# A seventeenth home for the experts' weights: the buffer of transposed rows becomes one, and the last gate row goes by DRAM

## The chip, the core and the metric

The kernel is one program on one core of a Trainium2 chip. The metric is device time in microseconds (us) of one execution, the median of three runs. A profiled execution, taken apart, gives the rows below. The engines are TensorE (PE; PEld is its weight load), VectorE (DVE), ScalarE (ACT), GpSimd (POOL) and SyncE (SP), which here issues nothing but DMAs.

## The reference, cut to what matters

Two layers of a diffusion transformer over 256 tokens of 1024 channels, all in float32. The even layer is attention with Fourier channel groups and then a dense SwiGLU; the odd layer is a gated short convolution and then eight expert SwiGLUs, of which each token uses two:

```
probs = softmax(h @ router); vals, idx = top_k(probs, 2); wts = vals / sum(vals)
combine = sum(one_hot(idx, 8) * wts[..., None], axis=-2)
for e in range(8):
    out = out + combine[..., e:e+1] * ((silu(h @ w_gate[e]) * (h @ w_up[e])) @ w_down[e])   # 1024 x 3584, 3584 x 1024
x = x + gate2 * rmsnorm(out, g_post)
```

The last line needs a "gate row": the modulation gate times the norm's weight, 1024 numbers, the same for every token. All of the experts' weights are read once: 8 experts of 42 MB (here and below 1 MB is 2^20 bytes, 128 partitions by 8 KB).

## The kernel before, in words

**The stream.** All weights lie in DRAM as units of 2 MB (128 partitions by 4096 floats) in the order of their use. SP loads them one after the other. In the dense layers a unit goes into one of the seven slots of `ring`. An expert has 21 units: 14 of gate and up weights (`gate_up`), then 7 of down weights (`down`). Here units are split in halves of 1 MB, p0 to p41, and each half has a *home*: `HOME[p]`. Homes 0 to 13 are the halves of the ring's seven slots; homes 14 and 15 lie in `wide_acc`, a buffer that the dense layers use for other things. `home_at` gives a home's place.

**How a home comes free.** TensorE signals `given_back[home]` when it has used a half: for the even half in the middle of the unit's work, for the odd half with the first matmul of the next unit. SP waits for `given_back` of a home before it loads the next half into it (L438 in the expert loop), strictly in the order p0, p1, ... Nothing later can go ahead of a half whose home is still in use. The table says which half of the expert used the home before. With 16 homes the table is 0 to 15, then 0 to 3, 6 to 15, 4, 5, 6 to 15: so p20 (home 6) waits for p6, p30 (home 4) for p4, p32 (home 6) for p20. Units listed in `BY_HALVES` are loaded by two DMAs of 1 MB (L413) and TensorE waits for each half apart; all others by one DMA of 2 MB (L410), which waits for both homes and for which TensorE waits at the start of the unit. Before, units 7, 8, 14, 19 and 20 go by halves.

**The experts.** The number of tokens of an expert selects the width of its code: 64, 96, 128, 144 and so on (`ARMS`). Each width has its own unrolled code; after each expert TensorE branches to the next width's code. With the inputs of this case the tiles in the trace show the widths 64, 96, 144, 64, 128, 64, 96, 64 for experts 0 to 7. Widths 64 and 96 are "narrow": tokens are the stationary side (L1953 for gate and up, L1995 for down). Wider ones keep the weights stationary (L1928). ACT computes silu into `gated_e` (L760) and DVE multiplies it with the up half (L1316). `gated_e` is the first 1024 floats of `hT`; `hT` (2048 floats per partition, exactly one home) otherwise holds the transposed rows of the layer's input, whose last reader is the router's matmul (semaphore `logit_ps`, L1806).

**The gate rows.** `gg` is the last 2048 floats of `wide_acc`: gate rows for the third and the fourth norm. The first of them is read in `add_y(2, b)` before the experts begin, the second in `add_y(3, b)` at the very end (L1030). Home 15 overlaps the first.

**Order around the change.** Home 14's first load waits for `red_ps` 13, home 15's for the gather matmuls (`gather_ps` 4), with which the experts begin. During an expert POOL fetches the next one's rows; in the last expert it fetches the experts' results from `y_store`, in two steps (`fetch_results`, L541).

## Time and profile before

| | us |
|---|---|
| median of 3 runs | 1436.09 (1435.29 to 1437.74) |
| the profiled execution | 1438.39 |
| its span, first to last instruction | 1436.6 |
| PE busy | 1387.9 (97%) |
| weight load busy | 979.0 (68%) |
| DVE, ACT, POOL busy | 462.6, 269.3, 49.2 |
| moved by DMA | 490.45 MB, mean 341 GB/s |

PE is shown busy nearly all the time, but its ends are modelled: a PE that is paced by the weights' arrival looks busy too. The waits of PE, the rate of the DMA engines and the moments at which SP issues the loads say more. The experts take the time from 522.6 to about 1425 us.

### The profile page before, as it was taken

To read this page: it belongs to the slowest core of one execution; us is meant where nothing else is said; L and a number is where in the kernel's file an instruction comes from. 1 tells how busy PE (TensorE), PEld (TensorE's weight loads), DVE (VectorE), ACT (ScalarE), POOL (GpSimd) and SP (SyncE) were. 2 spreads that over 40 slices of the span, in tenths; PEclk is the share of its full clock that TensorE was granted. 3 is DMA by queue.
4 is the path that set the end of the run, shared out by engine and by line. 5 is a ranking of instruction groups with operands and counts; after the bars stand their busy time and mean duration, and the time that the engine had idled before them with its cause. 6 is when DMAs were issued, how large, how long until landed. Compare 5 with 4: busy or idle time off the path is not lost.

```text
span 1436.6 us, 24598 instructions
## 1 busy us (share of the span) xinstructions
PE 1387.9 (97%) x10446; PEld 979.0 (68%) x10446; DVE 462.6 (32%) x759; ACT 269.3 (19%) x557; POOL 49.2 (3%) x63
## 2 busy tenths in 40 slices
PE   7999999998999999899999999999999999999896
PEld 4456599973598576366489954658994795664782
DVE  3587787777477341111000000101000111110122
ACT  3245321110300132111110000311000221110221
POOL 1000000000100012000000000000000000000000
PEclk9999999999999999999999999999999999999998
DMA  9977766660698679999996587999979999999995
GB/s 380 383 298 292 267 233 238 257 237 0 270 427 343 257 270 421 423 424 425 417 416 243 216 323 286 386 424 426 425 278 396 381 426 425 424 415 419 423 425 237
DMA packets 47531, 490.45 MB, mean 341 GB/s; under 512 B 7091, under 2 KB 7827, under 8 KB 13888
## 3 DMA queue, kind: packets, MB, share of 16 engines
q1 hardware_dynamic: 39136, 468.96, 80.0%
q0 software_dynamic: 6624, 17.08, 3.1%
q10 hardware_dynamic: 1664, 2.75, 0.5%
q8 instruction: 95, 1.56, 0.4%
q14 instruction: 12, 0.10, 0.0%
HBM read 480.83 MB, written 13.26 MB: 344 GB/s over the span
## 4 chain that ended last, share of the span: by engine, by line
PE 85%; DMA 8%; DVE 4%; ACT 1%; issue 1%; SPq 0%; DVEq 0%; ACTq 0%
PE ps L1953 24%; PE ps L1928 15%; PE ps L1995 14%; PE ps L1629 9%; DMA ring<-stream 7%; PE ps L1742 5%; PE ps L1665 4%; PE ps L1394 3%; PE ps L1576 2%; DMA hTe<-ctx_in 2%; PE ps L1911 1%; DVE acc L885 1%; PE ps L1494 1%; PE ps L1456 1%; PE ps L1510 1%
## 5 line engine op out<-in xcount | busy, mean ns | idle before, releaser
L1953 PE MATMUL ps<-ring,hTe 128*64 128x256 f32 (+1 forms) x3328 | 339.7, 383 | 13.5 <-issue 9.4
L1953 PEld LDWEIGHTS ps<-ring,hTe 128*64 128x64 f32 (+1 forms) x3328 | 234.4, 131 | 99.2 <-issue 23.6
L1316 DVE TENSOR_TENSOR aT<-hT,ps 128x512 f32<-128x512 f32 x112 | 77.1, 688 | 547.1 <-ACT hT L760 541.4
L1995 PE MATMUL ps<-ring,aT 128*32 128x256 f32 (+2 forms) x1120 | 207.3, 507 | 4.9 <-DMA ring<-stream 4.9
L1928 PE MATMUL ps<-hTe,ring 128*128 128x144 f32 (+1 forms) x1664 | 195.7, 281 | 2.1 <-DMA ring<-stream 2.1
L1928 PEld LDWEIGHTS ps<-hTe,ring 128*128 128x128 f32 x1664 | 195.1, 191 | 3.8 <-DMA ring<-stream 3.0
L1995 PEld LDWEIGHTS ps<-ring,aT 128*32 128x32 f32 (+2 forms) x1120 | 82.0, 133 | 122.7 <-issue 104.8
L760 ACT ACTIVATE hT<-ps 128x512 f32<-128x512 f32 x112 | 66.9, 597 | 458.5 <-PE ps L1953 273.6
L885 DVE SCALAR_TENSOR_TENSOR acc<-ring,silu_c,acc 128x1024 f32<-128x1024 f32 x80 | 102.6, 1282 | 2.9 <-DMA ring<-stream 0.9
L1742 PE MATMUL ps<-hT,ring 128*128 128x256 f32 (+1 forms) x480 | 83.9, 337 | 0.0
L1995 PE MATMUL ps<-acc,aT 128*64 128x512 f32 (+2 forms) x448 | 83.4, 503 | 0.0
L1742 PEld LDWEIGHTS ps<-hT,ring 128*128 128x128 f32 x480 | 76.2, 191 | 7.9 <-issue 0.5
L1258 DVE TENSOR_SCALAR hTe<-ps,ab 128x256 f32<-128x256 f32 x28 | 13.3, 537 | 188.8 <-PE ps L1840 188.8
L1629 PE MATMUL ps<-hT,ring 128*128 128x128 f32 x528 | 61.2, 275 | 0.2 <-issue 0.2
L1995 PEld LDWEIGHTS ps<-acc,aT 128*64 128x64 f32 (+2 forms) x448 | 32.9, 133 | 41.7 <-issue 38.1
L1629 PEld LDWEIGHTS ps<-hT,ring 128*128 128x128 f32 x528 | 60.0, 192 | 1.0 <-issue 1.0
L753 ACT ACTIVATE aT<-ps 128x512 f32<-128x512 f32 x84 | 49.8, 593 | 17.5 <-PE ps L1911 17.4
L731 ACT ACTIVATE hTe<-ps,ab 128x256 f32<-128x256 f32 x28 | 13.5, 564 | 167.7 <-PE ps L1840 167.7
L1629 PE MATMUL ps<-xn,acc 128*128 128x128 f32 x352 | 43.0, 275 | 0.6 <-DVE xn L1016 0.6
L1629 PE MATMUL ps<-xn,ring 128*128 128x128 f32 x352 | 43.0, 275 | 0.0
L1911 PE MATMUL ps<-cst,aT 128*64 128x128 f32 (+1 forms) x448 | 42.2, 273 | 0.0
L1394 PE MATMUL ps<-ring,hT 128*128 128x512 f32 x96 | 42.1, 593 | 0.0
(278 smaller groups left out, 1129.6 us busy)
## 6 DMA issues: line engine op xcount, KB each, us to landing
ring<-stream SPq DMA_DIRECT2D x182, 2048.0 KB, 14.8
acc<-stream SPq DMA_DIRECT2D x48, 1024.0 KB, 16.6
ring<-stream SPq DMA_DIRECT2D x32, 1024.0 KB, 16.1
y_store<-aT POOLq DMA_DIRECT2D x1, 8192.0 KB, 28.2
acc<-norm_w POOLq DMA_DIRECT2D x4, 512.0 KB, 18.2
y_store<-acc ACTq DMA_DIRECT2D x10, 128.0 KB, 9.3
x<-x_in SPq DMA_DIRECT2D x1, 1024.0 KB, 5.3
hTe<-ctx_in SPq DMA_DIRECT2D x1, 1024.0 KB, 22.9
```

The costliest lines, as they stand in the source:

```text
L753: act.activation(aT_e[:, u, :, :].rearrange("p b n -> p (b n)"), ps[:, 6 + u % 2, :], ACT.Copy).then_inc(eT_ok, 1)
L760: act.activation(gated_e[:, u % 2, :, :], ps[:, q:q + 2, 0:SEQ], ACT.Silu).then_inc(e_silu, 1)
L885: last = dve.scalar_tensor_tensor(out=dst, in0=slot(what)[:, k * D:(k + 1) * D][:, cols], scalar=silu_c[:, 4 * h + k, 0:1], in1=dst, op0=A ...
L1316: dve.tensor_tensor(aT_e[:, u, :, :], gated_e[:, u % 2, :, :], ps[:, q:q + 2, SEQ:2 * SEQ], ALU.mult).then_inc(e_a, 1)
L1394: last = pe.matmul(ps[:, blk, :], lhs[:, k, b * P:(b + 1) * P], w[:, k, :], start=(k == 0), stop=(k == KD - 1))
L1629: last = pe.matmul(ps[:, gu_bank(u, x), i * P:(i + 1) * P], w[:, i, k * P:(k + 1) * P], tokens[:, k, :], start=(x in (1, 2, 5, 7) and i == ...
L1665: last = pe.matmul(ps[:, bank, :], lhs[:, k, :], w[:, k, :], start=(d == 0 and k == 0), stop=(d == DOWNS - 1 and k == n - 1))
L1742: last = pe.matmul(ps[:, bank, c + t0:c + t1], w[:, i % 4, k, :], hT[:, k, t0:t1], start=(k == 0), stop=(k == KD - 1))
L1911: last = pe.matmul(ps[c:c + tile, 6 + u % 2, b * 256:b * 256 + P], aT_e[:, u, b, c:c + tile], ident, start=True, stop=True)
L1928: last = pe.matmul(ps[:, 2 * (u % 2) + b, g * SEQ:g * SEQ + width], w, hTe[:, k, 0:width], start=(k == 0), stop=(k == KD - 1))
L1953: last = pe.matmul(to, hTe[:, k, s0:s0 + n], w, start=(k == 0), stop=(k == KD - 1))
L1995: last = pe.matmul(ps[n * r:n * (r + 1), bank, 0:cols], a_T, w[:, part * cols:(part + 1) * cols], start=(j == 0), stop=(j == NFE - 1))
```

## The change

Seventeen homes. Homes 0 to 13 stay; home 14 stays; home 15 is now `hT` as a whole; home 16 is the former home 15. `gated_e` moves from `hT` to the last 1024 floats of `wide_acc`, where the fourth norm's gate row was. That row is therefore written to DRAM (`gate_store`) once it is ready, and read back, broadcast to all partitions (512 KB), into the place of home 0 in the last expert, after home 0's last use. ACT waits once for the write before its expert loop. The table of homes is new: 0 to 16, then 0 to 3, 9 to 16, 4 to 8, 9 to 16. Because 17 is odd, pairs of homes no longer fall on whole units: now units 4, 7, 8, 9, 10 and 13 to 20 go by halves, 13 of 21 in place of 5.

```diff
-HOME = [0, 1, 2, 3, 4, 5, 6, 7, 8, 9, 10, 11, 12, 13, 14, 15,
-        0, 1, 2, 3, 6, 7, 8, 9, 10, 11, 12, 13, 14, 15, 4, 5,
-        6, 7, 8, 9, 10, 11, 12, 13, 14, 15]
+HOME = [0, 1, 2, 3, 4, 5, 6, 7, 8, 9, 10, 11, 12, 13, 14, 15, 16,
+        0, 1, 2, 3, 9, 10, 11, 12, 13, 14, 15, 16, 4, 5, 6, 7, 8,
+        9, 10, 11, 12, 13, 14, 15, 16]
...
-BY_HALVES = [u for u in range(PER_EXPERT) if HOME[2 * u] >= 2 * RING or u in (2 * RING // 2 + 1, PER_EXPERT - 2)]
+BY_HALVES = [u for u in range(PER_EXPERT)
+             if HOME[2 * u] % 2 or HOME[2 * u + 1] != HOME[2 * u] + 1 or HOME[2 * u + 1] >= 2 * RING
+             or STAYS[HOME[2 * u]] != STAYS[HOME[2 * u + 1]]]
...
-        gated_e = hT[:, 0:4, :].rearrange("p (r k) t -> p r k t", r=2)
+        gated_e = wide_acc[:, 7 * D:8 * D].rearrange("p (r k t) -> p r k t", r=2, k=2)
...
         def home_at(home):
+            if home == 2 * RING + 1:
+                return hT[:, :, :].rearrange("p k t -> p (k t)")
             if home >= 2 * RING:
-                at = (0, 5 * D)[home - 2 * RING]
+                at = 0 if home == 2 * RING else 5 * D
...
+        last_gate = home_at(0)[:, 0:D]
...
                 elif home == 2 * RING:
                     sp.wait_ge(red_ps, 13)
+                elif home == 2 * RING + 1:
+                    sp.wait_ge(logit_ps, 2)
...
+            pool.wait_ge(red_ok, 10)
+            pool.dma_start(gate_store, gg[0:1, 1, :]).then_inc(gate_kept, 16)
...
             fetch_results(y_sum, 0, y_back)
+            pool.wait_ge(given_back[0], E * STAYS[0])
+            pool.wait_ge(gate_kept, 16)
+            pool.dma_start(last_gate, gate_store.to_broadcast([P, D])).then_inc(gate_back, 16)
             pool.wait_ge(e_ps, E * GU_UNITS)
             fetch_results(y_more, 1, y_more_back)
...
+            act.wait_ge(gate_kept, 16)
...
+                gates = last_gate if post == 3 else gg[:, post % 2, :]
+                if post == 3 and b == 0:
+                    dve.wait_ge(gate_back, 16)
```

Two places of the program show how the order moves. The first is SP in expert 0, from p16 on (the loop over the later experts has the same order). Before, `given_back6` and `given_back7` are waited for by p20 and p21, `given_back10` and `11` by p24 and p25:

```order
L413 DMA ring<-stream 128x2048 [waits given_back0]
L413 DMA ring<-stream 128x2048 [waits given_back1]
L410 DMA ring<-stream 128x4096 [waits given_back3,given_back2]
L410 DMA ring<-stream 128x4096 [waits given_back7,given_back6]
L410 DMA ring<-stream 128x4096 [waits given_back9,given_back8]
L410 DMA ring<-stream 128x4096 [waits given_back11,given_back10]
L410 DMA ring<-stream 128x4096 [waits given_back13,given_back12]
L413 DMA acc<-stream 128x2048 [waits given_back14]
L413 DMA acc<-stream 128x2048 [waits given_back15]
L410 DMA ring<-stream 128x4096 [waits given_back5,given_back4]
```

The same place with the change, from p16 on; `given_back15` is now `hT` and `given_back16` the second home in `wide_acc`:

```order
L420 DMA acc<-stream 128x2048 [waits gather_ps,rows_free]
L420 DMA ring<-stream 128x2048 [waits given_back0]
L420 DMA ring<-stream 128x2048 [waits given_back1]
L420 DMA ring<-stream 128x2048 [waits given_back2]
L420 DMA ring<-stream 128x2048 [waits given_back3]
L420 DMA ring<-stream 128x2048 [waits given_back9]
L417 DMA ring<-stream 128x4096 [waits given_back11,given_back10]
L417 DMA ring<-stream 128x4096 [waits given_back13,given_back12]
L420 DMA acc<-stream 128x2048 [waits given_back14]
L420 DMA hT<-stream 128x2048 [waits given_back15]
L420 DMA acc<-stream 128x2048 [waits given_back16]
L420 DMA ring<-stream 128x2048 [waits given_back4]
```

The row behind `given_back3` waits for home 9 now (p21 for p9), where before it was home 6 (p20 for p6); homes 4 to 8, free by then, are only loaded from p29 on. The row that waits for homes 10 and 11 loads p22 and p23 now, and loaded p24 and p25 before.

The second place is POOL at the end of the program, before and with the change. `xn` takes the first results, `hTe` the second:

```order
L541 DMA xn<-y_store,row_at 128x1024 [waits returned,gather_ps]
L541 DMA xn<-y_store,row_at 128x1024
L541 DMA hTe<-y_store,row_at 128x1024 [waits e_ps]
L541 DMA hTe<-y_store,row_at 128x1024
L139 UNCONDITIONAL_BRANCH
```

```order
L552 DMA xn<-y_store,row_at 128x1024 [waits returned,gather_ps]
L552 DMA xn<-y_store,row_at 128x1024
L562 DMA ring<-gate_store 128x1024 [waits gate_kept,given_back0]
L552 DMA hTe<-y_store,row_at 128x1024 [waits e_ps]
L552 DMA hTe<-y_store,row_at 128x1024
```

The gate row's read stands between the two fetches, behind home 0's last use (p17, in unit 8 of the last expert).

## Rows read from the trace of the kernel before

**Rows 1.** PE's waits in the whole span, longest in total first.

```profile
PE ps L1953 <- issue: 9.4, 3, 3.7
...
PE ps L1995 <- DMA ring<-stream: 4.9, 4, 2.0
PE ps L1953 <- DMA ring<-stream: 4.1, 1, 4.1
...
PE ps L1928 <- DMA ring<-stream: 2.1, 1, 2.1
```

**Rows 2.** Busy time, clock, DMA share, GB/s in windows, one an expert.

```profile
core 0: us, PE busy (x) PEld busy (x) DVE busy (x) ACT busy (x) POOL busy (x), PEclk, DMA share, GB/s
522.60:600.80 78.20, 77.81 (x632) 44.88 (x632) 15.27 (x35) 18.60 (x34) 15.69 (x24) 1.00 0.98 392
605.00:725.80 120.80, 120.80 (x1361) 66.95 (x1362) 12.92 (x20) 18.80 (x34) 1.99 (x2) 0.99 1.00 422
725.80:899.60 173.80, 173.80 (x1250) 138.81 (x1252) 12.92 (x20) 12.77 (x21) 1.98 (x2) 1.00 0.74 289
899.60:977.20 77.60, 77.60 (x632) 44.64 (x632) 12.82 (x20) 19.73 (x35) 1.98 (x2) 1.00 1.00 416
979.30:1129.50 150.20, 150.18 (x1026) 123.07 (x1028) 12.83 (x20) 12.07 (x21) 1.99 (x2) 1.00 0.93 377
1129.50:1207.20 77.70, 77.70 (x632) 64.96 (x632) 12.73 (x20) 19.71 (x35) 1.98 (x2) 1.00 1.00 417
1210.20:1330.80 120.60, 120.56 (x1360) 66.78 (x1360) 12.92 (x20) 19.01 (x34) 0.00 (x0) 0.99 1.00 420
1334.50:1425.00 90.50, 83.37 (x624) 63.35 (x624) 15.61 (x22) 17.19 (x30) 3.78 (x4) 0.96 0.93 392
```

**Rows 3.** The chain that ended last: three expert boundaries and the end.

```profile
578.15 26.00 DMA ring<-stream
604.15 0.83 issue
...
955.48 23.79 DMA ring<-stream
979.32 0.71 PE ps L1928 x4
...
1185.45 23.25 DMA ring<-stream
1208.70 1.53 issue
...
1387.29 23.86 DMA ring<-stream
1411.19 3.65 PE ps L1995 x16
```

**Rows 4.** SP's issues at the start of expert 5 (start, us, count).

```profile
1137.38 0.33 SPq L410 DMA_DIRECT2D ring<-stream  x1
...
1144.73 0.33 SPq L410 DMA_DIRECT2D ring<-stream  x1
1148.39 7.68 SPq L410 DMA_DIRECT2D ring<-stream  x3
```

**Rows 5.** Issue to landing (us) of p24/p25: windows 545.0:545.2, 922:923, 1152:1153.

```profile
ring<-stream SPq DMA_DIRECT2D x1, 2048.0 KB, 13.2
...
ring<-stream SPq DMA_DIRECT2D x1, 2048.0 KB, 12.7
...
ring<-stream SPq DMA_DIRECT2D x1, 2048.0 KB, 11.7
```

**Rows 6.** The same for lone transfers: windows 757:766, 1122.5:1123, 1083.5:1093.

```profile
ring<-stream SPq DMA_DIRECT2D x2, 2048.0 KB, 9.3
...
ring<-stream SPq DMA_DIRECT2D x1, 2048.0 KB, 9.0
...
acc<-stream SPq DMA_DIRECT2D x2, 1024.0 KB, 5.1
```

**Rows 7.** Totals of windows 1223:1232 (2 MB loads) and 1240.3:1244.8 (1 MB loads).

```profile
DMA packets 262, 3.85 MB, mean 428 GB/s; under 512 B 27, under 2 KB 27, under 8 KB 27
...
DMA packets 260, 1.89 MB, mean 421 GB/s; under 512 B 29, under 2 KB 29, under 8 KB 29
```

**Rows 8.** Windows of 10 us early in expert 5 and late in expert 6.

```profile
1140.00:1150.00 10.00, 10.00 (x102) 9.95 (x100) 2.06 (x3) 3.25 (x6) 0.00 (x0) 1.00 1.03 435
1150.00:1160.00 10.00, 10.00 (x102) 9.95 (x100) 2.04 (x3) 3.26 (x6) 0.00 (x0) 1.00 1.00 426
1290.00:1300.00 10.00, 10.00 (x92) 3.81 (x84) 0.69 (x1) 1.68 (x3) 0.00 (x0) 1.00 0.92 365
1300.00:1310.00 10.00, 10.00 (x94) 3.87 (x93) 0.00 (x0) 0.00 (x0) 0.00 (x0) 1.00 1.03 433
```

**Rows 9.** PE in the last expert's last three units.

```profile
1411.19 3.65 PE L1995 MATMUL ps<-ring,aT 128*64 128x512 f32 x16 [1.62 <-DMA ring<-stream]
1414.77 3.70 PE L2014 MATMUL ps<-xn,cst 128*128 128x512 f32 x8
1418.40 3.65 PE L1995 MATMUL ps<-ring,aT 128*64 128x512 f32 x16
1421.89 3.60 PE L1995 MATMUL ps<-acc,aT 128*64 128x512 f32 x16
```

**Rows 10.** PE's waits for "issue" where the last expert begins.

```profile
1334.52 2.80 PE L1953 MATMUL ps<-ring,hTe 128*64 128x256 f32 x22 [3.70 <-issue]
1339.96 6.17 PE L1953 MATMUL ps<-ring,hTe 128*64 128x256 f32 x41 [2.65 <-issue]
```

More of the change, by code:

```diff
@@ L167, in build @@
         y_store = nc.dram_tensor("y_store", (SEQ * E, D), F32).ap()
+        gate_store = nc.dram_tensor("gate_store", (1, D), F32).ap()
         slot_table = nc.dram_tensor("slot_table", (SEQ * E, 2), F32).ap()
@@ L272, in build @@
             sem(n) for n in ("table_empty", "entries_ok", "table_s", "rows_out", "lists_in", "token_at_ok", "rows_back"))
-        stored = sem("stored")
+        stored, gate_kept, gate_back = sem("stored"), sem("gate_kept"), sem("gate_back")
         gu_done, gu_sum, snap, c_ok = sem("gu_done"), sem("gu_sum"), sem("snap"), sem("c_ok")
@@ L1029, in add_y @@
                     cols = slice(h * BANK, (h + 1) * BANK)
-                    dve.tensor_tensor(xn[:, b, cols], y_bank(post, b)[:, h, :], gg[:, post % 2, cols], ALU.mult)
+                    dve.tensor_tensor(xn[:, b, cols], y_bank(post, b)[:, h, :], gates[:, cols], ALU.mult)
                 roots[0] += 1
```

## The prediction, made before the changed kernel ran

> **What bounds the kernel now.** I read PE's waits first [rows 1]. In 1436.6 us it waits for weights by name only 4.9 + 4.1 + 2.1 = 11.1 us, and 9.4 us for "issue". Then a window for each expert [rows 2]: the reader is to see two kinds. In experts 2 (width 144) and 4 (width 128) the DMA engines move 289 and 377 GB/s while PE works without a gap: PE sets the pace, and SP waits for homes. In the others they move 416 to 422 GB/s at a DMA share of 1.00 (experts 0 and 7, at 392, contain their own ramp and end). A width-64 expert takes PE about 77.7 us for 42 MB, that is 1.85 us a MB, but 2^20 bytes at 425 GB/s take 2.47 us: there the weights fall behind by some 26 us, which the loaded homes have to cover. The chain of waits [rows 3] shows that they just do not: at the ends of experts 0, 3 and 5 it goes through a weight DMA and the next expert starts late (at 979.32 straight from a landing, at 604.15 and 1208.70 a landing plus 0.83 and 1.53 us of issue), and in the last expert it goes through a landing at 1411.15. So there are three stretches in which every microsecond of delay of the weights is a microsecond of the kernel: A, expert 0 up to the start of 1; B, expert 3 up to the start of 4; C, from expert 5 to the end. Elsewhere PE is the bound and more homes change nothing.
>
> **What 17 homes ought to give.** One more MB loaded when a stretch begins is 2.47 us of DMA time, three times: 7.4 us. Whether it reaches the stretch's end depends on whether the DMA engines stay busy in between, and this is where the new table matters.
>
> **The table at the start of a width-64 expert.** Both tables load the first expert's halves without waiting for one another; then PE eats faster than homes refill. Before, p20/p21 wait for p6/p7, issued at 1144.73 [rows 4], and the next three 2 MB loads are issued from 1148.39 on at (7.68 - 0.33) / 2 = 3.67 us apart: 1148.39 (homes 8, 9), 1152.06 (homes 10, 11), 1155.73 (homes 12, 13). These are the moments at which PE frees those homes, and they don't move. Now p21 alone waits for home 9, 1148.39; p22/p23 wait for homes 10 and 11, 1152.06; p24/p25 for homes 12 and 13, 1155.73. Each is 2 MB further back in the stream than what stood there before, and homes 4 to 8 lie empty until p29. By 1149 the engines have nothing left: before, p18/p19, issued at 1137.38 [rows 4], land like p24/p25 some 11.7 us later [rows 5], at about 1149; now the seventeenth home lets the engines start 1 MB earlier, which puts p20, the last before p21, at about the same moment. So p21 runs alone, landing 5.1 us after issue [rows 6] at 1153.5, and p22/p23, issued 1.4 us before that, are almost alone too: 9.3 us to landing, 1161.4, then p24/p25 one transfer of 2 MB later: 2 x 2.444 = 4.89 us by the 428 GB/s of [rows 7] (1.0486 / 0.428 = 2.45 us a MB). From the same issue moment that is 9.3 + 4.9 = 14.2 us, against 13.2, 12.7 and 11.7 us measured for p24/p25 in experts 0, 3 and 5 [rows 5]. The same half of the stream lands **1.0, 1.5 and 2.5 us later** than before, in spite of the extra home. With the lone transfer at 9.0 us (the other row in [rows 6]) it is 0.3 us less each. From there to the stretch's end the engines run without a break in both kernels, so the difference stays. As bounds: if p20 to p23 in fact queue up and none is lone, nothing is lost and up to 2.5 us a stretch gained; if p22/p23 start only when p21 has landed (1153.5 + 9.3 + 4.9 = 1167.7 against 1163.8), 3.9 us are lost.
>
> **More transfers of 1 MB.** Thirteen units by halves in place of five: 16 MB more of each expert in 8 KB rows. 1 MB costs 1.0486/0.421 = 2.49 us so, and 2.45 in 2 MB loads [rows 7]; with the rounding of the rates 0.04 to 0.05. Of the tail of a stretch (p26 to p41) 10 MB change form: 0.5 us in A, 0.5 in B, 0.5 in C for expert 5; all of experts 6 and 7 adds 0.8 each. C: 2.1 us. Bounds 0 and twice that.
>
> The Trainium skill ("DMA: Bandwidth & Descriptors", section "Anatomy of one DMA") puts a fixed cost of about 2.0 us on each DMA beside its bytes. Taken one by one that would be 8 x 2.0 = 16 us an expert. The trace has it for a lone load (5.1 us for 1 MB, 9.3 for 2 MB, [rows 6]), but in a full queue a row of 1 MB loads still moves 421 GB/s [rows 7], so it is covered there; it is only paid where the queue runs dry, which is the step above.
>
> **The gap in expert 6.** At 1290 to 1300 the rate is 365 GB/s [rows 8], 10 x (1 - 365/425) = 1.4 us of idle: p36/p37 waited there for the pair of units 12/13. Now p36 waits for p23, a pair earlier; the gap goes: **-1.4 us** (bounds 0 and -1.4).
>
> **The gate row.** Its write (4 KB) is issued by POOL between two issues that wait far apart, ACT waits for it long after; nothing. The read moves 512 KB into SBUF while stretch C's weights run: 0.524 MB at 425 GB/s = **+1.2 us** on the stream's end (it is issued when unit 9 begins, about 1372). The second result fetch behind it on POOL waits for the end of gate and up, 1387, so isn't held up. What if PE's last units had slack: then 0, the lower bound.
>
> **Finer waits at the end.** PE now waits for p36 at unit 18 and for p37 half a unit later. The wait that ends at 1411.19 [rows 9] was for a whole unit; half of that unit's work, 3.65 / 2 = 1.8 us, now goes ahead of the landing. Behind it stand 3.6 + 3.6 + 3.6 us without a wait, and the last half was due at 1421.89 + 1.8: the last landing then becomes equally tight. **-1.8 us** (bounds 0 and -1.8). Units 0, for which the starts of experts 1, 4 and 6 wait, are whole in both.
>
> **Others at nothing.** `gated_e` elsewhere: the same ACT and DVE instructions. Home 15 can be filled from `logit_ps` on (before the gathers): its 2.5 us lie in a DMA pause, and this is the extra MB of stretch A already counted. PE's code grows by a net one instruction for each width.
>
> **Sum.** A: 1.0 + 0.5 = 1.5. B: 1.5 + 0.5 = 2.0. C: 2.5 + 2.1 - 1.4 + 1.2 - 1.8 = 2.6. Together +6.1; with the lone transfer at 9.0 us, 0.9 less: +5.2. In A part of the delay may hide in the 0.83 us of issue behind the landing. I take **+5.1 us**. The profiled execution took 1438.39 us (span 1436.6 and 1.8 around it), which becomes 1443.5; the median of the runs, 2.3 us below the profiled one, goes from 1436.09 to **1441.2**. A measurement of this kernel can tell about 0.2%, 2.9 us, from no change.
>
> **Rival 1: the extra home pays (faster).** If the engines don't run dry at p21, each stretch gains 2.47 us less the packets: A -2.0, B -1.6 (its wait was 2.1 in all, less 0.5), C -2.5 + 2.1 - 1.4 + 1.2 - 1.8 = -2.4: 1430.1. For it speak the waits, which exist; against it, that the issue moments of [rows 4] are PE's, and the new order reads from the table. It would decide where p20 lands later than 1150. Chance 0.14.
>
> **Rival 2: they cancel.** The delay at p24/p25 is nearer 0 to 1 us, because traffic that slows the weights in the first 15 us of an expert (results stored, rows gathered) now falls into the idle time: A 0.5, B 0.5, C 0.5 + 2.1 - 1.4 + 1.2 - 1.8 = 0.6: +1.6, 1437.7. For it: p24/p25 in expert 0, where most such traffic is, comes out as the smallest delay. Chance 0.24.
>
> **Rival 3: code loading (much slower).** PE waits 3.70 and 2.65 us for "issue" as the last expert begins [rows 10], neither for a landing. The change shifts the code by an instruction per width and adds halves' waits. A pause of 3.7 us more at each of the three starts 1, 4 and 6 would give 5.1 + 11.1: 1452.3. Against it: experts 3 and 5 start without any pause, and the pauses lie at branches that are the same. The Trainium skill ("Runtime: NRT & Kernel Launch", "Instruction fetch mechanics") says that a taken branch out of the loaded blocks waits for a fetch of the target; the pauses at the last expert agree, and by that rule an instruction more changes nothing unless a block's edge is crossed. Chance 0.06.
>
> **How the numbers follow.** Forecast 0.56, rivals 0.14, 0.24, 0.06. The forecast's own range is 1438 to 1446 (the lost time 0.3 us less or 1.4 us more a stretch, the packets 0 or double). For 8 in 10 I go from 1433.5 to 1446.5: it leaves out the far half of rival 1, rival 3 and the forecast's upper edge. Slower by over 2.9 us (1439.0): 0.51 of the forecast, rival 3 and 0.04 of rival 2: 0.61. Same: the rest of the forecast 0.05, 0.19 of rival 2 and 0.03 of rival 1: 0.27. Faster: 0.12.
>
> **What the profile after would show.** At the start of experts 3 and 5: SP issues a 1 MB load some 18.9 us after the expert's start, then 2 MB loads 3.67 us apart; in the windows of 10 us there, a rate 20 to 30% below 425 between 14 and 24 us after the start, where 435 and 426 stand in [rows 8]; p24/p25 landing about 14 us after issue. PE's wait at the start of expert 4 near 4 us in place of 2.1. No dip late in expert 6. A wait of PE in the last units of experts 0, 3 and 5. The prediction is wrong if that dip is absent or if the start waits of experts 1, 4 and 6 shrink; wrong in its size if p24/p25 lands within 12 to 13 us.

## The result

| us | before | changed |
|---|---|---|
| median | 1436.91 (4 runs, 1435.29 to 1438.31) | 1447.62 (4 runs, 1447.37 to 1450.86) |
| the profiled execution | 1438.39 | 1447.71 |
| its span | 1436.6 | 1445.9 |

The ratio is 1.0074, 95% interval 1.0058 to 1.0089: 10.7 us slower. The forecast was +5.1 us and its range ended at 1446.5: the direction was right, the size was not.

PE's waits after, to be read against [rows 1] ("issue" is time in which PE waited for nothing that the profile shows):

```profile
PE ps L1971 <- issue: 11.3, 4, 4.8
...
PE ps L1971 <- DMA ring<-stream: 5.1, 1, 5.1
PE ps L2013 <- DMA ring<-stream: 4.5, 5, 1.8
PE ps L1946 <- DMA ring<-stream: 3.5, 1, 3.5
```

L1971, L2013 and L1946 are the former L1953, L1995 and L1928. Each of the three waits at an expert's start has grown: 4.1 to 5.1 at expert 1, 2.1 to 3.5 at expert 4, and 3.0 to 4.8 (put down to issue) at expert 6. One window for each expert, as in [rows 2]:

```profile
522.90:600.80 77.90, 77.67 (x633) 44.77 (x632) 15.25 (x35) 18.68 (x34) 15.69 (x24) 1.00 0.95 374
606.10:726.80 120.70, 120.66 (x1361) 66.95 (x1361) 12.92 (x20) 17.85 (x33) 1.98 (x2) 0.99 1.01 422
...
900.70:978.90 78.20, 77.61 (x632) 44.56 (x632) 12.81 (x20) 19.72 (x35) 1.97 (x2) 1.00 0.97 394
982.90:1135.50 152.60, 152.60 (x1024) 125.53 (x1024) 12.82 (x20) 11.69 (x20) 1.98 (x2) 0.98 0.93 371
1135.50:1215.10 79.60, 78.41 (x633) 60.97 (x632) 12.82 (x20) 19.71 (x35) 1.98 (x2) 1.00 0.97 395
```

The reader is to see the last column: in experts 0, 3 and 5 the rate fell from 392, 416 and 417 GB/s to 374, 394 and 395. The weights are the bound there and the DMA engines now stand still for part of the time. The row of expert 4 tells something else: 152.6 us in place of 150.2 with a mean clock of 0.98.

SP's issues at the start of expert 5, as in [rows 4]. The row x5 ends with p21 (20.5 us after the start; 19.2 in expert 3), the row x2 is p22 to p25:

```profile
1138.09 18.26 SPq L420 DMA_DIRECT2D ring<-stream  x5
1159.74 4.00 SPq L417 DMA_DIRECT2D ring<-stream  x2
1165.09 0.33 SPq L420 DMA_DIRECT2D acc<-stream  x1
```

Windows of 10 us there (15 us behind the start) and late in expert 6, against [rows 8]:

```profile
1150.50:1160.50 10.00, 10.00 (x102) 9.11 (x100) 2.06 (x3) 3.26 (x6) 0.00 (x0) 1.00 0.73 275
...
1300.00:1310.00 10.00, 10.00 (x91) 3.84 (x84) 0.69 (x1) 1.68 (x3) 0.00 (x0) 1.00 1.01 419
```

The dry spell that was forecast is there (275 GB/s), and the gap late in expert 6 is gone. The same 10 us of experts 0 and 3 are alike, the kernel before first and then the changed one:

```profile
537.50:547.50 10.00, 10.00 (x100) 6.86 (x98) 2.06 (x3) 2.79 (x6) 3.19 (x6) 1.00 1.01 428
914.50:924.50 10.00, 10.00 (x100) 6.82 (x98) 2.06 (x3) 2.81 (x6) 0.00 (x0) 1.00 1.01 433
```
```profile
537.90:547.90 10.00, 10.00 (x100) 6.82 (x98) 2.06 (x3) 2.78 (x6) 5.56 (x11) 1.00 0.65 224
915.60:925.60 10.00, 10.00 (x100) 6.82 (x98) 2.06 (x3) 3.01 (x6) 0.00 (x0) 1.00 0.77 269
```

In the last expert PE waits by halves, as against [rows 9]:

```profile
1417.30 1.94 PE L2013 MATMUL ps<-ring,aT 128*64 128x512 f32 x8 [0.54 <-DMA ring<-stream]
1419.79 1.94 PE L2013 MATMUL ps<-ring,aT 128*64 128x512 f32 x8 [0.55 <-DMA ring<-stream]
1422.25 1.94 PE L2013 MATMUL ps<-ring,aT 128*64 128x512 f32 x8 [0.53 <-DMA ring<-stream]
```

Two things were not forecast. Early in expert 5 PE stands after 22 matmuls, in the middle of a unit, for no landing:

```profile
1135.54 2.80 PE L1971 MATMUL ps<-ring,hTe 128*64 128x256 f32 x22
1139.54 4.69 PE L1971 MATMUL ps<-ring,hTe 128*64 128x256 f32 x41 [1.20 <-issue]
```

Unit 2's first matmul comes 8.9 us after the expert's start, where it was 7.3: 1.6 us later, and so are the homes that come free behind it. And at the start of expert 4, behind the wait of 3.5 us, the granted clock is 0.50 (the lower level, 1.2 GHz). Windows of 2 us:

```profile
982.00:984.00 2.00, 1.12 (x5) 1.12 (x6) 0.00 (x0) 1.28 (x1) 0.00 (x0) 0.50 1.01 419
...
986.00:988.00 2.00, 2.00 (x12) 2.00 (x11) 0.00 (x0) 0.00 (x0) 0.00 (x0) 0.50 1.03 431
988.00:990.00 2.00, 2.00 (x18) 2.00 (x18) 0.00 (x0) 0.00 (x0) 0.00 (x0) 0.91 1.02 432
```

The spell lasts from 981.5 to 988.4, and 5.5 us of it lie behind the first matmul of expert 4 (982.9). Work at half the clock for 5.5 us loses 2.7: that is the 2.6 us by which expert 4 is longer (start to start 152.7 against 150.1).

### The profile page after: what moved, and what is told of

Its sections match the earlier page's. It is cut to its first block, busy times and chain, and to the rows that moved or that the text cites. A ratio compares the mean times of both kernels' runs of the same rounds, so it can differ in the third digit from the quotient of the medians.

```text
span 1445.9 us, 24722 instructions
## 1 busy us (share of the span) xinstructions
PE 1392.4 (96%) x10446; PEld 977.9 (68%) x10446; DVE 462.7 (32%) x759; ACT 269.2 (19%) x557; POOL 50.3 (3%) x65
## 4 chain that ended last, share of the span: by engine, by line
PE 84%; DMA 9%; DVE 4%; ACT 1%; issue 1%; SPq 0%; DVEq 0%; ACTq 0%
PE ps L1971 24%; PE ps L1946 15%; PE ps L2013 14%; PE ps L1647 9%; DMA ring<-stream 7%; PE ps L1760 5%; PE ps L1683 4%; PE ps L1412 3%; PE ps L1594 2%; DMA hTe<-ctx_in 2%; PE ps L1929 1%; DVE acc L900 1%; PE ps L1512 1%; PE ps L1474 1%; PE ps L1528 1%
## 5 line engine op out<-in xcount | busy, mean ns | idle before, releaser
L1971 PE MATMUL ps<-ring,hTe 128*64 128x256 f32 (+1 forms) x2944 | 309.7, 385 | 16.4 <-issue 11.3
L1971 PEld LDWEIGHTS ps<-ring,hTe 128*64 128x64 f32 (+1 forms) x2944 | 208.6, 132 | 98.2 <-issue 25.9
L1334 DVE TENSOR_TENSOR aT<-acc,ps 128x512 f32<-128x512 f32 x112 | 77.0, 688 | 553.5 <-ACT acc L775 550.7
L2013 PE MATMUL ps<-ring,aT 128*32 128x256 f32 (+2 forms) x1120 | 208.7, 504 | 4.5 <-DMA ring<-stream 4.5
L1946 PE MATMUL ps<-hTe,ring 128*128 128x144 f32 (+1 forms) x1472 | 176.8, 283 | 3.5 <-DMA ring<-stream 3.5
L1946 PEld LDWEIGHTS ps<-hTe,ring 128*128 128x128 f32 x1472 | 175.7, 193 | 5.1 <-DMA ring<-stream 4.3
L2013 PEld LDWEIGHTS ps<-ring,aT 128*32 128x32 f32 (+2 forms) x1120 | 82.4, 133 | 120.7 <-issue 97.3
L775 ACT ACTIVATE acc<-ps 128x512 f32<-128x512 f32 x112 | 66.9, 597 | 469.8 <-PE ps L1971 279.8
L2013 PE MATMUL ps<-acc,aT 128*64 128x512 f32 (+2 forms) x336 | 66.8, 503 | 0.8 <-DMA acc<-stream 0.8
L768 ACT ACTIVATE aT<-ps 128x512 f32<-128x512 f32 x84 | 49.8, 593 | 17.5 <-PE ps L1929 17.4
L1971 PE MATMUL ps<-acc,hTe 128*64 128x256 f32 (+1 forms) x384 | 47.5, 380 | 0.0
L2013 PEld LDWEIGHTS ps<-acc,aT 128*64 128x64 f32 (+2 forms) x336 | 24.0, 133 | 33.0 <-issue 26.7
```

The source lines that it names most:

```text
L768: act.activation(aT_e[:, u, :, :].rearrange("p b n -> p (b n)"), ps[:, 6 + u % 2, :], ACT.Copy).then_inc(eT_ok, 1)
L775: act.activation(gated_e[:, u % 2, :, :], ps[:, q:q + 2, 0:SEQ], ACT.Silu).then_inc(e_silu, 1)
L1334: dve.tensor_tensor(aT_e[:, u, :, :], gated_e[:, u % 2, :, :], ps[:, q:q + 2, SEQ:2 * SEQ], ALU.mult).then_inc(e_a, 1)
L1946: last = pe.matmul(ps[:, 2 * (u % 2) + b, g * SEQ:g * SEQ + width], w, hTe[:, k, 0:width], start=(k == 0), stop=(k == KD - 1))
L1971: last = pe.matmul(to, hTe[:, k, s0:s0 + n], w, start=(k == 0), stop=(k == KD - 1))
L2013: last = pe.matmul(ps[n * r:n * (r + 1), bank, 0:cols], a_T, w[:, part * cols:(part + 1) * cols], start=(j == 0), stop=(j == NFE - 1))
```

## The experiments

Differences are from the median of the kernel before in the same comparison, which lay at 1436.7 to 1438.7 us; ratios are of the runs of the kernel to the runs of the kernel before, with their 95% interval. The changed kernel is +10.7. In the diffs + and - are against the changed kernel where nothing else is said. Its `BY_HALVES` is worked out from `HOME`, so a new table also changes which units go by halves: 13 of them in the changed kernel, 3 in a16, 15 in k1, 13 in k2, 14 in c17 and 15 in t17.

### Is it the table? a16, bhalf, anogate, lighta, lightb

**a16**:

```diff
-HOME = [0, ..., 16, 0, 1, 2, 3, 9, ..., 16, 4, ..., 8, 9, ..., 16]
+HOME = [0, ..., 15, 0, 1, 2, 3, 6, ..., 15, 4, 5, 6, ..., 15]
```

> The changed kernel with the table of sixteen homes of the kernel before; the second home outside the ring is hT, and the gate row still goes by DRAM. Theory (the table alone is the cause): as the kernel before plus 1.2 us of the gate row's read, 1438.1 us, 1436.5 to 1439.5; start of expert 4 with a wait of about 2 us and no spell at clock 0.50; expert 5 begins without a pause for issue. Rival (the gate row, hT as a home or the shifted code cost): 1442 us or more, with the pause at the start of expert 5.

1440.19 us, +2.3; 1.0015 (1.0000 to 1.0030). The table, with the halving that follows from it, takes 8.4 of the 10.7 us away. A little above the expected range. In its trace PE stands 3.48 us at the start of expert 4, put down to issue, where the two profiles of the kernel before wait 2.1 and 1.6 us for weights; there is no pause in expert 5.

**bhalf** (against the kernel before):

```diff
-BY_HALVES = [u for u in range(PER_EXPERT) if HOME[2 * u] >= 2 * RING or ...]
+BY_HALVES = [4, 7, 8, 9, 10, *range(13, 21)]
```

> The kernel before, its table kept, with 13 units by halves in place of 5 (units 4, 7 to 10 and 13 to 20), the same as in the changed kernel. Theory (1 MB transfers cost 0.04 to 0.05 us each where the queue is full, and the finer waits at the end give back 1.8): 0.5 + 0.5 + 2.1 - 1.8 = 1.3 us more than before, 1438.2 us, 1436 to 1440. Rival (1 MB transfers carry what the prediction missed): 1442 us or more. If the code's shift by more waits makes the pause in expert 5, it shows here too.

1437.53 us, -0.4; 1.0001 (0.9987 to 1.0015). The 1 MB transfers cost nothing that can be measured, a little less than forecast. No pause in expert 5.

**anogate**:

```diff
-            pool.dma_start(last_gate, gate_store.to_broadcast([P, D])).then_inc(gate_back, 16)
...
-                    dve.wait_ge(gate_back, 16)
```

> The changed kernel without the read of the gate row; the last norm multiplies with whatever lies in home 0, so this part of the output is not the reference's. Theory (the read of 0.5 MB takes 1.2 us of the weights' stream in the last expert): 1446.4 us, 1445 to 1447. Rival (it is hidden): 1447.6. Rival (it costs much more, because it is written to 128 partitions and stands ahead of the second fetch of results): below 1444.

1446.85 us, +9.6; 1.0068 (1.0052 to 1.0085). This kernel leaves out the read of the gate row. Its median is 0.8 us below the changed kernel's (1.1 if each is taken from its own kernel before) where 1.2 was expected; the intervals overlap, so it only shows that the read is not large.

**lightb** and **lighta** (the same edit on the kernel before and on the changed one; every load of the experts' weights leaves out half of its columns):

```diff
-                    sp.dma_start(ring[:, ring_slot(HOME[p]), :], stream[..., :, :],
+                    sp.dma_start(ring[:, ring_slot(HOME[p]), 0:HALF], stream[..., :, 0:HALF],
...
-                sp.dma_start(home_at(HOME[p]),
+                sp.dma_start(home_at(HOME[p])[:, 0:HALF // 2],
```

> The kernel before with the loads of the experts' weights cut to half their columns in the same way; output not the reference's. Theory: 1410 to 1425 us, the same as lighta within 1.5 us; the waits for issue (9.4 us before) shrink where the queue is light. Rival on those waits (they belong to the branches and don't depend on the queue): they stay at 3 us or more each at the starts of experts 1, 6 and 7.

> The changed kernel with every load of the experts' weights cut to half its columns, so half of each expert's weights are old numbers and the output is not the reference's; the same number of DMAs, waits and matmuls. Theory (nothing but the arrival of the weights separates the two kernels): the same time as lightb within 1.5 us; both have no wait for weights in the experts, 1410 to 1425 us; what is left of PE's waits for issue at the starts of experts shows how much of them comes from the loaded queue. Rival (moved buffers, gate row, code): lighta 3 us or more above lightb.

1417.15 and 1416.32 us; 0.9850 (0.9833 to 0.9868) and 0.9847 (0.9829 to 0.9865). With the weights out of the way the two kernels are equal within what can be measured (intervals of 2.6 us to either side): the moved buffers and the code show no cost of their own. PE has no wait for weights in the experts, and its waits for issue in lighta, from 520 us on, are

```profile
PE ps L1971 <- issue: 4.5, 2, 2.8
```

against 11.3 in the changed kernel, and 5.2 in lightb against 9.4. So about 1416 us is what is left when no table makes PE wait for weights, and about half of the waits put down to issue come only beside a full DMA queue.

### Which entry of the table? k1, k2, c17, t17

**k1** and **k2**, one and two homes moved forward:

```diff
-HOME = [*range(17), *range(4), *range(9, 17), *range(4, 9), *range(9, 17)]
+HOME = [*range(17), *range(5), *range(9, 17), *range(5, 9), *range(9, 17)]    # k1
+HOME = [*range(17), *range(6), *range(9, 17), *range(6, 9), *range(9, 17)]    # k2
```

> The changed kernel with one entry of the table moved: home 4 goes from p29 to p21, and homes 9 to 16 move up by one (0 to 16, 0 to 4, 9 to 16, 5 to 8, 9 to 16). p21 then waits for p4, used long before, and p22 waits for p9. Theory (p21's wait for p9 and the dry spell behind it make the three stretches late): no dry spell, p24/p25 land 2 to 4 us earlier after each start, 1439 us, 1436 to 1442. Rival (seventeen homes cost in any order, through the moved buffers, the gate row or the code): 1445 us or more. Rival (only the wrap from one expert to the next counts, as it did with the table of c17, where p4 waited for p33): no change from 1447.6.

> The same with homes 4 and 5 moved up to p21 and p22 (0 to 16, 0 to 5, 9 to 16, 6 to 8, 9 to 16). Theory: p23 is the first to wait for p9, and by then the engines still have three loads queued; p4 and p5 of the next expert still wait for halves 25 loads back. Each stretch gains something of the seventeenth home over the kernel before: 1436 us, 1433 to 1439. Rival: as k1, 1445 us or more; or equal to the kernel before, 1438.

k1: 1441.90 us, +4.7; 1.0031 (1.0019 to 1.0042). k2: 1436.93 us, -0.3; 0.9999 (0.9990 to 1.0008). One home takes back 6.0 us, two take back 11.0: all of the loss. The halving can't be the reason: k1 sends the same 15 units by halves as a11 below, which has the changed kernel's table and takes 1450.79 us (+12.1), and k2 has 13 such units like the changed kernel (unit 11 for unit 13). The same 10 us of expert 5, from about 15 us behind its start, in k1, in k2:

```profile
1147.90:1157.90 10.00, 10.00 (x102) 9.08 (x100) 1.91 (x3) 3.26 (x6) 0.00 (x0) 1.00 0.98 386
```
```profile
1140.10:1150.10 10.00, 10.00 (x102) 9.06 (x100) 2.06 (x3) 3.26 (x6) 0.00 (x0) 1.00 1.02 424
```

275 GB/s became 386 and then 424, the rate of the kernel before.

**c17**:

```diff
+HOME = [*range(17), 0, 1, 2, 3, *range(4, 12), 12, 13, 14, 15, *range(4, 12), 16]
```

> The changed kernel with another table of seventeen homes: 0 to 16, 0 to 3, 4 to 11, 12 to 15, 4 to 11, 16, so that p21 waits for p4 and every load up to p32 reuses the home of the load 17 before it. Theory (the loss comes from the order of the homes: p21 waits for p9 and the DMA engines run dry there): no dry spell, the seventeenth home pays 2.47 us less the 1 MB transfers in each stretch, PE's wait at the start of expert 4 falls below 1 us and with it the spell at clock 0.50; 1431 us, 1428 to 1434. Rival (the 1 MB transfers, here nearly all, or the gate row are what costs): 1445 us or more. Rival (the seventeenth home is worth nothing in any order): 1437.

1455.44 us, +17.5; 1.0122 (1.0094 to 1.0149): wrong by 24 us. The rival that named such a time, the 1 MB transfers, is not the reason: aall below has more of them (all 21 units, here 14) and takes 1441.30. The table is a ring: behind p41 comes p0. In c17 home 4 is last used by p33, so p4 of the next expert waits for p33, 13 loads back, where in the changed kernel it waited for p29. SP's 2 MB loads at the end of expert 2, in c17 and in the kernel before:

```profile
843.14 55.41 SPq L415 DMA_DIRECT2D ring<-stream  x7
```
```profile
845.68 45.70 SPq L410 DMA_DIRECT2D ring<-stream  x7
```

The seven loads that should be a stock for the width-64 expert take 55.4 us to issue in place of 45.7, and p4/p5 goes out at 868.2 in place of 853.6. The order around p21 was mended and the order across the experts was broken.

**t17**, a table found by counting issue, arrival and use for each half with the durations of the trace:

```diff
+HOME = [*range(17), 0, 1, 2, 4, 3, 6, 7, 8, 11, 10, 14, 15, 16, 1, 12, 4, 5, 9, 8, 10, 11, 13, 14, 15, 16]
```

> The changed kernel with a table found by working the order of homes through a count of issue, arrival and use: 0 to 16, then 0, 1, 2, 4, 3, 6, 7, 8, 11, 10, 14, 15, 16, 1, 12, 4, 5, 9, 8, 10, 11, 13, 14, 15, 16; no home comes back in fewer than 12 loads where the engines could run dry. Theory (more of the seventeenth home's 2.5 us a stretch reaches the end than with k2): by that count 2 us below k2, 1435 us, 1432 to 1438. Rival (at the starts of experts 1, 5, 6 and 7 PE waits for issue anyway, as in k2, so earlier weights give nothing): 1437, as k2 and the kernel before.

1444.74 us, +6.0; 1.0045 (1.0029 to 1.0061): worse than k2, not better. The count knew nothing of waits for issue and clock. t17 has a pause of 3.1 us at the start of expert 2, one of 2.1 in expert 5, and spells at 0.50 that begin at 1400.3 and 1417.3 us, and the down units of its last expert wait 8.2 us for weights in seven pieces. Which part of the 6 us each of these is was not separated.

### Does a load of 2 MB make it worse? aall, a11

```diff
+BY_HALVES = list(range(PER_EXPERT))                        # aall
+BY_HALVES = [4, 7, 8, 9, 10, 11, 12, *range(13, 21)]       # a11
```

> The changed kernel, its table kept, with all 21 units by halves (in the changed kernel it was 13). Theory of the dry spell with its second part (a load of 2 MB, p22/p23, waits for both of its homes, so that behind the lone p21 the engines wait for home 11 too): p22 goes out when home 10 is free, half a unit earlier, PE too starts unit 11 on a half; some of the 9 us come back: 1442 us, 1440 to 1445. Rival (p21's wait alone sets it): 1447.6. Rival (1 MB transfers cost): above 1449.

> The changed kernel with units 11 and 12 by halves too (15 of 21); p22 to p25 are the four halves behind the lone p21. Theory (the wait of a 2 MB load for the later of its two homes lengthens the dry spell, and those two units are the whole of what halving all units gave, 6.3 us): p22 goes out 1.7 to 1.9 us after p21 in place of 3.7, PE's wait at the start of expert 4 falls under 2.5 us and the spell at clock 0.50 goes: 1442 us, 1440.5 to 1443.5. Rival (the gain of halving all is spread over PE's finer waits in all units): 1445.5 us or more.

aall: 1441.30 us, +4.1; 1.0034 (1.0019 to 1.0048), as expected. a11: 1450.79 us, +12.1; 1.0078 (1.0060 to 1.0097): no gain, against the theory. The landing of p25 (the sixteenth and last update of its load's semaphore, the same as in [rows 5]), counted from the start of expert 3, where no kernel has a pause, says how much of it is the dry spell (us; expert 5 beside it):

```
                       expert 3   expert 5
before                 35.4       34.4
before2                34.4       34.7
changed                36.1       37.9
after2                 36.9       38.7
ap128                  36.6       38.3
a11                    36.7       40.4
aall                   36.2       35.5
k1                     33.5       34.9
k2                     32.6       36.5
c17                    44.6       44.3
```

In expert 3 a11 and aall land p25 no earlier than the three profiles of the changed kernel's table above them, and unit 0 of expert 4 at 81.4 and 81.8 us against 82.2, 82.9 and 82.3. So of the second part of the theory (a load of 2 MB waits for the later of two homes) at most some 1 us is left. Where aall gains can be seen: in it unit 0 goes by halves too, so that PE begins expert 4 at 79.3 us, before all of the unit has landed, and then waits 1.5 us for the rest; and in expert 5 the pause of the changed kernel is absent. In a11 that pause is longer, and the clock is down behind it:

```profile
1136.15 2.80 PE L1969 MATMUL ps<-ring,hTe 128*64 128x256 f32 x22
1141.52 6.25 PE L1969 MATMUL ps<-ring,hTe 128*64 128x256 f32 x41 [2.56 <-issue]
```
```profile
1143.00:1145.00 2.00, 2.00 (x13) 2.00 (x11) 0.10 (x1) 0.60 (x1) 0.00 (x0) 0.57 1.05 440
```

Expert 5 takes 87.0 us in a11 (82.4 in aall), and a11 also has a pause of 3.1 us at the start of expert 2.

### Pauses and clock: awarm, after2, before2, ap128, kp128

**awarm**:

```diff
                     pe.wait_ge(hTe_act, e * 4 + 4)
+                    if width == 128:
+                        for _ in range(20):
+                            pe.transpose(ps[:, 0, 0:P], ident, ident)
```

> The changed kernel with 20 transposes of the identity into an idle PSUM bank ahead of unit 0 in the code of width 128, which only expert 4 runs: PE works in its wait of 3.46 us for the weights. Theory (the wait before it lowers the granted clock in 981.5 to 988.4, and that costs expert 4 2.6 us, not the late landing alone): clock 1.00 throughout, L1946 in expert 4 back to about 100.3 us, 1445.0 us, 1444 to 1446. Rival (the weights are late in expert 4 anyway, so a faster PE only waits elsewhere, or the lower clock comes on its own): 1447.6 us.

1446.31 us, +8.4; 1.0058 (1.0041 to 1.0076). In its trace the spell at the start of expert 4 is gone and expert 4 takes 150.1 us again. The median fell by 1.3 us of the 2.6 (2.3 if each is taken from its own kernel before), with overlapping intervals: shown for the stretch, not for the whole.

**after2** and **before2** are the two kernels unchanged, one run each.

> The changed kernel again, for a second profile. Theory (the pause in the first unit of expert 5 and the spell at clock 0.50 at the start of expert 4 belong to the kernel): both are there again, within 0.5 us of 1.8 and 2.6 us; 1447.6 us. Rival (they are chance of the execution): one or both are gone or elsewhere, and the time moves with them.

> The kernel before again, for a second profile. Theory: no pause in expert 5, no spell at 0.50 in expert 4; waits for issue of 9.4 us in all, at the same places; 1437 us. Rival: they move by microseconds between executions.

1448.05 and 1435.43 us. The pause in expert 5 is there again in after2 (1.74 us) and absent again in before2. The spell in expert 4 is not: after2's first 10 us of expert 4, against those of the changed kernel's first profile,

```profile
984.90:994.90 10.00, 9.99 (x89) 9.99 (x90) 0.69 (x1) 1.69 (x2) 0.00 (x0) 1.00 1.02 429
```
```profile
982.90:992.90 10.00, 10.00 (x66) 10.00 (x67) 0.00 (x0) 0.92 (x1) 0.00 (x0) 0.73 1.01 426
```

though PE had waited 3.3 us there too. So the pause belongs to the kernel, and the spell comes in some executions and not in others: behind waits of 3.3 to 3.5 us it is in the changed kernel's first profile and in those of anogate and ap128, and not in after2.

**ap128**, **kp128** (on the changed kernel and on k2):

```diff
-                pe.addr_align(256, offset=0, max_nops=0)
+                pe.addr_align(256, offset=128, max_nops=0)
```

> The changed kernel with the first experts' code placed 128 instructions further from a boundary of 256 (nothing else is changed). Theory (the pause in expert 5 hangs on where the code lies): PE's waits for issue in the experts change by over 2 us in the sum and sit at other matmuls; 1443 to 1452 us. Rival (place of the code is without effect, pauses come from the loaded queue alone): as the changed kernel, 1447.6 within 1.5 us, pauses at the same places.

> k2 with its first experts' code moved in the same way. Theory: the 2.2 us pause in expert 5 and the 3.7 us one at expert 1 move or go, 1434 to 1441 us. Rival: 1437 as k2.

ap128: 1448.89 us, +12.2; 1.0069 (1.0048 to 1.0091). kp128: 1436.53 us, -0.2; 0.9989 (0.9974 to 1.0003). The pause in expert 5 stays in both (1.66 and 1.94 us). But at the start of expert 1 the wait changed its size and its kind, k2 and kp128:

```profile
603.00 9.23 PE L1969 MATMUL ps<-ring,hTe 128*64 128x256 f32 x76 [3.74 <-issue]
```
```profile
599.80 3.67 PE L1969 MATMUL ps<-ring,hTe 128*64 128x256 f32 x32 [1.38 <-DMA ring<-stream]
605.62 1.73 PE L1969 MATMUL ps<-ring,hTe 128*64 128x256 f32 x14 [2.15 <-DMA ring<-stream]
```

In k2 unit 0's load was issued at 579.98 and took 21.2 us:

```profile
ring<-stream SPq DMA_DIRECT2D x1, 2048.0 KB, 21.2
```

So the weights were there at 601.2. PE, free since 599.3, stood until 603.0: the first half of that wait is the weights', and the second is put down here to its own code, whose fetch (a packet of the instruction queue) had begun at 600.3. In kp128 PE waits 1.38 us for the landing alone, but then 2.15 us more for the next unit's weights: what the pause covered, the weights take. Each is one profile.

### Both ends together: k2all, kpall

```diff
+BY_HALVES = list(range(PER_EXPERT))     # on k2 and on kp128
```

> k2 (homes 4 and 5 moved up to p21 and p22) with all 21 units by halves. Theory (finer loads and waits take away the pause of 2.2 us in the first unit of expert 5 and the spell at clock 0.50 behind it, as in aall against the changed kernel, and shorten what dry time is left): 1433.5 us, 1431 to 1436, faster than k2 and the kernel before. Rival (the pause in expert 5 goes with the table; PE waits for issue at the starts of experts 1, 6 and 7 whatever the weights do): 1437 us as k2.

> The same with the first experts' code moved by 128 instructions, which in kp128 made the wait at the start of expert 1 1.4 us in place of 3.7. Theory: that much less again than k2all, 1432 us, 1430 to 1435. Rival: 1436.5 us as kp128.

k2all: 1435.07 us, -3.5; 0.9984 (0.9974 to 0.9993). kpall: 1435.52 us, -3.0; 0.9980 (0.9969 to 0.9990). Both are faster than the kernel before, by 2.3 to 3.5 us, a small difference that just clears the noise, and are the fastest kernels that ran with all of their weights. The pause in expert 5 is still there (1.84 us in both), so in aall it did not go with the halves alone; the start of expert 1 is free of waits (77.5 us after that of expert 0), with 2.0 and 1.2 us of waits for weights in its next two units.

## Why the prediction was wrong in size

The step that failed in size is the delay of the weights by the ends of experts 0, 3 and 5, which the sum took at 5.5 us (6.5, less 1.0 of deductions) and which measured 9.5. Two things that it had at nothing, the pause in expert 5 and the granted clock, are in the measured time as well.

**"The table at the start of a width-64 expert": right, and taken too small.** The issue moments were forecast as 18.9 us after the start for p21 (found: 19.2 in expert 3; 20.5 in expert 5, where the pause comes in) and 3.7 us apart behind it; the rate fell by a third in experts 3 and 5 and by a half in expert 0. In the first two profiles of each kernel p24/p25 lands later by 0.6 to 2.5 us in expert 0, 0.7 to 2.5 in expert 3 and 3.2 to 4.3 in expert 5, against 1.0, 1.5 and 2.5. Counted as the prediction counted, from the issue of p22/p23, it lands 13.2 to 14.9 us later ("about 14 us"). What counts is unit 0 of the next expert. Its landing, from the expert's start, us:

```
                    expert 0        expert 3        expert 5
before, before2     81.6 81.2       79.8 79.3       79.3 79.6
changed, after2,    82.7 83.7       82.2 82.9       83.2 84.2
  ap128             84.9            82.3            83.5
```

The means differ by 2.4, 2.9 and 4.2 us, together 9.5, where the prediction had 1.5, 2.0 and (2.5 + 0.5) = 3.0, together 6.5, before it took 0.9 off for a faster lone transfer and 0.1 for the issue behind the landing. Those deductions were the wrong way. Of the other 3.0 us that are missing 0.9 each are in experts 0 and 3, and 1.2 in expert 5, where the pause below is more than that. k1 and k2 show that the table is the cause of the whole loss, and in k2 the stream of expert 3 is ahead of the kernel before (p25 at 32.6 against 35.4 and 34.4), which is the seventeenth home at work.

**The pause in expert 5: not foreseen in the form it took.** Rival 3 spoke of pauses at the starts of 1, 4 and 6 and gave them 0.06; this one is in the first unit of expert 5. PE stands 1.20 us in the first profile and 1.74 in the second, and unit 2 begins 1.6 and 2.1 us later. It is in the 4.2 above, for it shifts the release of the homes behind it. Where it comes from is only partly known. bhalf and the changed kernel send the same 13 units by halves and show the same 10446 matmuls, and one has it and the other not; moving the first experts' code by 128 instructions left it; aall, c17 and a16 don't have it, k1, k2, t17, a11, awarm, anogate, k2all and kpall do. So moving the code is not enough to remove it, and the profiles with half the loads (lighta, lightb) don't show it. In the trace's records of the instruction queue each of the six profiles with full loads and no pause has a fetch at -0.1 to +0.4 us from the start of expert 5, and each of the twelve with it has that fetch at +1.6 to +2.7. What sets that moment stays open.

The page's row of that queue in the changed kernel, packets and MB:

```profile
q8 instruction: 95, 1.56, 0.4%
```

The Trainium skill ("Runtime: NRT & Kernel Launch", "Instruction fetch mechanics") says that an engine's code is fetched in blocks of 16 KiB by a DMA queue that its sequencer drives, that this is mostly hidden while the code runs straight on, and that a taken branch out of the loaded blocks waits for a fetch of its target. The blocks agree (each of the 95 packets has 16384 bytes), and so does the branch: the starts of experts 1, 6 and 7 that are put down to issue come 2.7 to 2.9 us behind a fetch in nearly every profile. Other starts are like that too: in the first profile of each kernel the start of expert 1, put down to the DMA, comes 2.7 us behind a fetch and 0.6 to 0.8 us behind unit 0's landing, where expert 4 starts within 0.1 us of its landing.

**The clock: not in the sum at all.** A spell at 0.50 cost expert 4 2.6 us in the first profile; after2 has none there and is no faster. How much of the 10.7 us of the medians is the clock stays open: the spells at 0.50 in the experts add up to 20.5, 17.1, 23.9 and 23.9 us in changed, after2, ap128 and anogate, against 13.7 and 20.5 in before and before2. The means are 4.3 us apart, and half of that, 2.1 us, is an estimate of what the clock can have cost at most by these profiles, since part of the spells lies in waits.

**"More transfers of 1 MB" and "Finer waits at the end".** bhalf has both on the old table: forecast 0.5 + 0.5 + 2.1 - 1.8 = +1.3, measured -0.4 (-1.9 to +2.2). Not told apart from the forecast, and the packets' price is at most small. The prediction's remark that the trace has a fixed 2.0 us for a lone load doesn't hold as it stands: the section that it cites is about DMAs that GpSimd issues, and [rows 6], less the bytes at 428 GB/s, leave 2.6 us for the 1 MB loads (which were issued two at a time) and 4.4 for 2 MB. No term of the sum used it.

**"The gap in expert 6", "The gate row".** The gap went (419 GB/s). The gate row cost 0.8 by medians, not clear of the noise, for 1.2. From the start of expert 6 to the end of the span the changed kernel took 225.9 us, before 226.4: -0.5, where the steps of that part summed to 1.6 - 1.4 + 1.2 - 1.8 = -0.4.

**"What 17 homes ought to give" and rival 1.** k2 shows the home at work in the stream, and yet k2 is only level. What the weights give, the starts take back in part: in k2 unit 0 of expert 1 landed 79.6 us after the start of expert 0 in place of 81.6 and 81.2, yet expert 1 began after 81.4 in place of 82.5 and 81.3, 2.7 us behind its code's fetch; and in expert 5 the pause takes 2.2 us. So these tables did not bring rival 1's -2.0, -1.6 and -2.4; k2all got 2.3 to 3.5 us of its 6.

By the starts of the experts the first pair of profiles differs by +0.4 (before expert 0) + 0.8 (A) - 0.1 (experts 1 and 2) + 2.5 (B) + 2.6 (expert 4's clock) + 3.6 (expert 5, with the pause) - 0.5 (the rest) = 9.3 us, which is 1445.9 - 1436.6. The second pair differs by +2.5 + 3.5 - 0.8 + 3.6 + 0.0 + 4.5 - 0.8 = 12.6 us by its spans (the terms, rounded, add up to 12.5). What both pairs show is the loss in A, B and expert 5, 6.8 and 11.7 us; the time before expert 0 is chance, for the same kernel reached it at 519.4 and at 522.5 us.

## What to carry to other kernels

A table of buffers is judged by the distance in loads between the one that used a buffer last and the one that takes it next, counted around the loop and across its end. What matters is not the smallest distance (12 before and changed, 11 in k2), but the distance where the queue has caught up with the consumer: the first load that has to wait there is 14 behind in the kernel before and in k2, 13 in k1 and 12 in the changed kernel (0, -0.3, +4.7 and +10.7 us). One more buffer in a worse order was 11 us slower, and moving two entries gave it all back. A strict order of loads makes one early wait stall all buffers that lie free behind it. When a wait for data shrinks, look at what was waiting under it (here code) before counting the gain.

## What was not expected of the hardware

- A taken branch: 2.7 to 2.9 us from the fetch's first packet to the next matmul beside a full DMA queue, and 2.67 us at the start of expert 7 in lighta and lightb. All waits put down to issue in the experts came to 7.5 to 17.3 us with full loads and 4.5 and 5.2 with loads cut to half.
- The granted clock was at 0.50 behind waits of 3.3 to 3.5 us in some executions and at 1.00 in others of the same kernel (the windows from 982.9 and from 984.9 us above).
- Sixteen loads of 1 MB in place of eight of 2 MB for each expert changed the time by -0.4 us, within what can be measured.
